# Moving the two moving operands' rows to 208 and 240 bytes from the weights' place within 256 bytes

## What is computed

```
def first_block(x, ...):
    hn = rmsnorm(h, norm_mix_g)
    proj = hn @ w_in + b_in
    ...
    y_m = hm @ w_branch_m
    y_c = (cb * causal_dwconv(cc * ch, conv_w)) @ w_branch_c
    merged = jax.nn.sigmoid(gm_pre) * y_m + jax.nn.sigmoid(gc_pre) * y_c
    h = h + merged @ w_out
    hn = rmsnorm(h, norm_ffn_g)
    u = causal_dwconv(hn @ w_up, ffn_conv_w, ffn_conv_b)
    gate, val = jnp.split(u, 2, axis=-1)
    h = h + (jax.nn.silu(gate) * val) @ w_down

def second_block(x, meta_tokens, ...):
    h = jnp.concatenate([meta, x], axis=1)          # 16 + 256 tokens
    u = rmsnorm_2(h, norm1_g[l])
    proj = u @ w_in[l]
    ...
    h = h + merged @ w_out[l]
    u2 = rmsnorm_2(h, norm2_g[l])
    h = h + jnp.square(jax.nn.relu(u2 @ mlp_w1[l])) @ mlp_w2[l]
    return rmsnorm_2(h, final_g)[:, N_META:]
```

## Time and profile before

| | |
|---|---|
| median of 3 runs | 2867.69 us |
| the three runs | 2854.05, 2867.69, 2872.25 us |
| the profiled execution | 2872.45 us |
| its span | 2870.7 us |
| instructions | 53265 |
| TensorE matmuls | 22994, busy 96% of the span |
| VectorE, ScalarE busy | 60%, 45% |
| mean granted TensorE clock | 0.979 |

### The profile page before, as it was taken

One profiled execution on the slowest core, in us unless ns is written; L12 is line 12 of the kernel. 1 busy time (PEld: TensorE's weight loads), 2 busy tenths in 40 slices (PEclk: granted clock), 3 DMA queues, 4 the chain that ended last, 5 costly groups with the idle time before them and its releaser, 6 DMA issues.

```text
span 2870.7 us, 53265 instructions
## 1 busy us (share of the span) xinstructions
PE 2744.2 (96%) x22994; PEld 2721.2 (95%) x22994; DVE 1711.4 (60%) x1725; ACT 1300.1 (45%) x1449; POOL 1.8 (0%) x14
## 2 busy tenths in 40 slices
PE   4988999999999999999999967999999999999998
PEld 4987999999999999999989967999999999999998
DVE  4544565566667567657785648755665555455555
ACT  3443454444554355445544375444454334343443
POOL 0000000000000000000000000000000000000000
PEclk9988999999999999999999988999999999999999
DMA  4442555555555555555545424555556565655653
GB/s 154 162 146 93 195 193 192 190 191 191 187 194 180 197 182 196 198 191 165 173 165 171 154 98 132 191 185 182 190 179 189 189 182 187 191 183 185 186 183 115
DMA packets 257814, 503.17 MB, mean 175 GB/s; under 512 B 10150, under 2 KB 19038, under 8 KB 257630
## 3 DMA queue, kind: packets, MB, share of 16 engines
q1 hardware_dynamic: 254592, 500.20, 53.1%
q10 hardware_dynamic: 3054, 0.55, 0.1%
HBM read 498.63 MB, written 2.10 MB: 174 GB/s over the span
## 4 chain that ended last, share of the span: by engine, by line
PE 87%; DVE 7%; ACT 4%; ACTq 1%; issue 1%; DVEq 0%
PE psum L461 27%; PE psum L462 27%; PE psum L463 26%; PE psum L485 2%; PE psum L486 2%; PE psum L487 2%; DVE wlo L1040 2%; DVE work L1068 1%; DVE work L1408 1%; ACT whi L727 1%; ACTq L713 1%; DVE misc L1454 0%; ACT misc L950 0%; DVE hn L1078 0%; DVE work L1439 0%
## 5 line engine op out<-in xcount | busy, mean ns | idle before, releaser
L1040 DVE TENSOR_TENSOR wlo<-raw,whi 128x1024 fp32r<-128x1024 f32 x952 | 1160.1, 1223 | 983.6 <-ACT whi L727 982.7
L727 ACT ACTIVATE whi<-raw 128x1024 fp32r<-128x1024 f32 x952 | 1003.3, 1058 | 1317.4 <-PE psum L463 1194.3
L461 PE MATMUL psum<-hn,whi 128*128 128x256 f32 x4448 | 1249.5, 281 | 38.9 <-DVE wlo L1040 25.9
L462 PE MATMUL psum<-hn,whi 128*128 128x256 f32 x4448 | 1247.0, 280 | 0.0
L463 PE MATMUL psum<-hn,wlo 128*128 128x256 f32 x4448 | 1246.7, 280 | 0.0
L461 PEld LDWEIGHTS psum<-hn,whi 128*128 128x128 f32 x4448 | 846.1, 190 | 42.6 <-DVE wlo L1040 28.9
L463 PEld LDWEIGHTS psum<-hn,wlo 128*128 128x128 f32 x4448 | 848.7, 191 | 0.0
L462 PEld LDWEIGHTS psum<-hn,whi 128*128 128x128 f32 x4448 | 842.5, 189 | 0.1
L461 PE MATMUL psum<-act,whi 128*128 128x256 f32 x2544 | 711.8, 280 | 14.8 <-DVE wlo L1040 9.3
L463 PE MATMUL psum<-act,wlo 128*128 128x256 f32 x2544 | 711.0, 279 | 0.0
L462 PE MATMUL psum<-act,whi 128*128 128x256 f32 x2544 | 710.9, 279 | 0.0
(11 more groups left out here) (207 smaller groups left out, 978.3 us busy)
## 6 DMA issues: line engine op xcount, KB each, us to landing
raw<-in_w_in SPq DMA_DIRECT2D x160, 1024.0 KB, 5.1
raw<-in_mlp_w SPq DMA_DIRECT2D x128, 1024.0 KB, 5.3
raw<-in_w_up SPq DMA_DIRECT2D x80, 1024.0 KB, 5.0
raw<-in_w_down SPq DMA_DIRECT2D x40, 1024.0 KB, 5.1
raw<-in_w_out SPq DMA_DIRECT2D x32, 1024.0 KB, 5.0
raw<-in_w_branch_m SPq DMA_DIRECT2D x8, 1024.0 KB, 5.0
raw<-in_w_branch_c SPq DMA_DIRECT2D x8, 1024.0 KB, 5.0
raw<-in_w_up SPq DMA_DIRECT2D x8, 768.0 KB, 4.4
```

Of the source, the lines that this page charges most:

```text
L461: mm(o, hi[:, kk, w], both[:, 0, :], start=first, stop=False)
L462: mm(o, hi[:, kk, w], both[:, 1, :], start=False, stop=False)
L727: A(whi[:, n % SLOTS, :], raw[:, n // 2 % RAW, n % 2 * HALF:(n % 2 + 1) * HALF], ACT.Copy)\
L1040: V.tensor_tensor(wlo[:, n % SLOTS, :], raw[:, n // 2 % RAW, n % 2 * HALF:(n % 2 + 1) * HALF], whi[:, n % SLOTS, :].bitcast(F32), ALU.subt ...
```

## The change

`hn` and `act` are allocated 8 elements (32 bytes) larger, and the names `hn` and `act` become views that begin 4 elements (16 bytes) into them. `act_flat` is cut from the tensor itself, and `view` is defined earlier in the code. Every later instruction names the same elements as before.

```
@@ -96,14 +96,24 @@
+        def view(t, at, *shape):
...
         raw = sb("raw", [P, RAW, CK * NC])
         whi = sb("whi", [P, SLOTS, HALF], F32R)
         wlo = sb("wlo", [P, SLOTS, HALF], F32R)
         h = sb("h", [P, NT, T])
 
         sb("gap_a", [P, 48])
-        hn = sb("hn", [P, NT, MAIN + 2 * T], F32R)
-        act = sb("act", [P, NT, 2 * T], F32R)
+        hn = view(sb("hn", [P, NT * (MAIN + 2 * T) + 8], F32R), 4, NT, MAIN + 2 * T)
+        act_flat = sb("act", [P, NT * 2 * T + 8], F32R)[:, 4:4 + NT * 2 * T]
+        act = view(act_flat, 0, NT, 2 * T)
...
-        act_flat = act[:, :, :].rearrange("p a b -> p (a b)")
```

More of the change, by code:

```diff
@@ L96, in sem, with view @@
             return sems[name]
+        def view(t, at, *shape):
+            n = 1
+            for s in shape:
+                n *= s
+            v = t[:, at:at + n]
+            if len(shape) == 2:
+                v = v.rearrange("p (a b) -> p a b", b=shape[1])
+            return v
         raw = sb("raw", [P, RAW, CK * NC])
@@ L124, in build @@
         psum = ctx.enter_context(nc.psum_tensor("psum", [P, 8, 512], F32))
[L126 to L133, removed]
         def col(name, i=0):
```

## The result

The kernel after takes 2911.98 us (median of 4 runs, 2905.29 to 2914.61), the kernel before 2865.29 us (median of 4, 2854.05 to 2872.25). The ratio is 1.0163, with a 95% interval of 1.0125 to 1.0201: slower by 1.6%, where 1.6% faster had been forecast. The time lies inside the stated range of 2800 to 2920 us, but that range took in both directions, and the kernel moved the other way.

A forecast was written before the change was run, and what follows sets the result against it. TensorE's matmul pace was taken as the bound. 2872.45 - 51.3 (113.3 ns pace everywhere) + 0 (wide stages) + 0 (VectorE, ScalarE) gave 2821 us, 1.6% below the median; range 2800 to 2920 us.

The forecast's parts named there:

- What bounds the kernel: Whole span: TensorE, busy 96%, sets the time; clock and DMA do not.
- Two locks drawn at each pause: Dense 256-column stretches: one instruction runs at 113.3 ns (fast) or 117.8 ns (slow), chosen by where TensorE restarts.
- The weight load as partner: Matmul stream: weight loads, TensorE's other reader of the same memory, likely form the pace pattern with the matmuls; no size.
- The worth of the locks: 20,976 matmuls on 256 columns: the 117.8 ns pace costs 51.3 us now, and 43.1 us more if everywhere.
- Between these ends I choose the fast lock everywhere: -51.3 us.: `hn` and `act` at new distances: every 256-column matmul at 113.3 ns, -51.3 us; chance 0.40.
- weak slope: Reason for the chosen direction: distance 128 costs 12.8 ns, 192 6.6 or 11.1, and 208 and 240 lie further off.
- The bound from above: `hn` and `act` at the pace of the 272-column stages (distance 128): 119.5 ns on 256 columns, 78 us more.
- The slow lock, or one like the wide stages', everywhere: Rival for `hn` and `act`: 117.8 ns everywhere, 2916 us, or the 272-column stages' pace, 2950 us; chance 0.29.
- The wide stages at 0: 1,536 matmuls of 272 columns, distance 128 to 144: taken as 0, between -9 and +9 us.
- VectorE, ScalarE and the register instruction at 0: Writes of `hn` and `act` 16 bytes on, and the instruction ahead of line 1063: no cost, 0 us.
- The rule that distance is worth nothing: Under the nothing-changes rival: the skill's two independent TensorE read ports make distance worth 0, 2868 us; rival's chance 0.25.

The follow-up runs named there:

- m1_places: Bare stream of 256-column matmuls, nothing else of the reference, moving row at sixteen distances from the weights: 113.3 to 120.0 ns per matmul.
- e3: Against the kernel after: weights moved 16 bytes on, `hn` and `act` back at distance 192 from them; 2819.06 us, ratio 0.9838.
- e5: Against the kernel after: `hn` and `act` both at distance 112, weights where they were; 2817.24 us, ratio 0.979.
- m3_weights_80_to_128: Bare matmul stream with weights 80, 96, 112 and 128 bytes from their place, each at all 16 distances; two equal-output cases 113.3 and 120.0 ns.
- m4_widths: Bare matmul stream with loads of 128 or 64 weight columns, 128 to 512 moving columns, five distances; at 256 columns 6.7 to 13.3 ns above bare.
- e6: Kernel with `hn` and `act` both at distance 96, 16 bytes nearer than in e5, weights where they were; 2948.86 us, ratio 1.0289.
- e4: Against the kernel after: weights moved 16 bytes on, `hn` and `act` kept at distances 208 and 240; 2931.38 us, ratio 1.0191.

## Why the prediction was wrong, point by point

**What bounds the kernel: right.** TensorE's pace does, and each kernel's time follows it: the span moved by 40.3 us where TensorE's busy time moved by 42.7.

**Two locks drawn at each pause: right.** m1_places shows both at distance 192 with pauses alone between, and the spread of the runs fits them: 24 us in 16 runs of before, 2 to 4 us in e3 and e5, which have one lock. Two details were misread. At 927 us the 0.18 us are lost inside one stage, where TensorE waits for the last part of `act` (VectorE line 1063), not for the operand of the next stage. And a change does not need a wait: at 740 us it came after eight float32 matmuls on `ones`, with TensorE busy all the time.

**The weight load as partner: right**, shown by the two cases of m3_weights_80_to_128 that differ in the weights' address alone (113.3 and 120.0 ns), and borne out by m4_widths.

**The worth of the locks: right.** The all-fast kernel was put at 2821 us. e3 measured 2819.06 and e5 2817.24.

**The step that failed: "Between these ends I choose the fast lock everywhere: -51.3 us."** Its reason was a weak slope, that 192 cost less than 128 and that 208 and 240 lie further from 128 on that side. There is no slope. The list jumps at each 16 bytes; with the weights at their place only 192 and 112 have anything below 116 ns, but for one stretch each at 16 and 64. The fast pattern "that holds itself" held at 192 and not one step away. In its place came 119.2 ns on `hn` and 117.2 on `act`. Worked out from the starts in both profiles, the mean pace rose from 115.8 to 118.9 ns on `hn` and from 115.9 to 117.2 on `act`: 13,344 x 3.1 + 7,632 x 1.3 ns = 41 + 10 = 51 us. Intervals of 200 ns and more between starts fell from 237 to 222 us, which gives the excess over 40 back: 9 us because 233 instead of 274 matmuls started 200 to 235 ns after the one ahead of them, the pace at a granted clock of 0.50, and 5 us by less time in intervals above 400 ns, the pauses. The matmuls that are no longer in such intervals take some 5 us at the ordinary pace, so 10 us remain of the 15. So TensorE's waits, which the change was said not to reach, shrank by some 5 us in these two profiles; why the clock stayed up a little more is open.

**The bound from above: right in size, for a reason that was doubtful.** By the wide stages it was 119.5 ns and 2950 us. The list's worst entry is 120.0 ns, and e6, which has it everywhere, measured 2948.86 us.

**The rival that came true, in part.** "The slow lock, or one like the wide stages', everywhere" gave 2916 to 2950 us, and 2911.98 was measured. It is not the slow lock of 117.8 ns: two other patterns took its place, 119.2 ns on `hn` and 117.1 on `act`, which average near it. That the sum came out 4 us below this rival's 2916 is in part luck. The evidence named for it was sound, that of the places in the trace only 192 showed 6.6 ns above the columns at all. With one good place known and none of its neighbours, the step away from it was more likely a loss than a gain, and the chances should have said so.

**The wide stages at 0: near.** Their mean pace went from 126.1 to 125.3 ns, 1 us in all. **VectorE, ScalarE and the register instruction at 0: right.**

**The rule that distance is worth nothing** fell with the runs. m1_places has 113.3 and 120.0 ns for one stream at two distances with every other engine idle; the two independent read ports that the Trainium skill gives TensorE ("SBUF — State Buffer", section "Who interferes with whom") do not account for that. The least that 256 columns showed is 113.3 ns, not the 109.2 that the Trainium skill has for isolated matmuls ("TensorE: Matmul & The Clock Gate", section "Back-to-back issue gap").

## What to carry to other kernels

Where matmuls with a weight load each run back to back, read the pace as time by count in several dense stretches; two values for one instruction mean that it stands on a pattern that restarts can change, and the spread of the runs is then a symptom too. Measure all sixteen distances between moving row and weights within 256 bytes, with the weights on and off the 32-byte grid, in one kernel that does nothing else, and carry the best entry over: here that list told the times of e5 and e6 to 3 and 8 us, though in e4 it missed a pace of 123.3 ns, and a guess from neighbouring entries told nothing. A list holds for its widths alone: with loads of 64 columns the best entry of this one becomes the worst.

## What the runs showed of the hardware that I had not expected

- The pace of a stream of 128-column loads and 256-column matmuls goes from 113.3 to 120.0 ns by the addresses alone, at clock 1.00 and with DMA, ScalarE and VectorE idle. It depends on the distance within 256 bytes and on the weights' place within 32, both measured in steps of 16 bytes.
- The patterns close after whole multiples of 16 periods of 2.4 GHz: 113.3 ns is 272 periods for one matmul, the slow lock 848 for three, that of `hn` after 2288 for eight (953.3 ns) and that of `act` 1968 for seven (820 ns). Which part of the memory or of the array has this step, no run shows.
- With 320 moving columns and loads of 128 all five distances gave 13.3 ns above the columns; with 384 and 512 they differed again, 13.3 to 23.4.
- In m4_widths TensorE worked for over 300 us, nearly without a pause, on loads of 128 with 128 moving columns, one every 213.3 ns, and the granted clock rose only at 341.49 us, after 32 matmuls on 192 columns. A pace read where the trace has no record of the clock yet can be that of the lower level, though the view writes 1.00.
